# Summing gathered rows with four column groups of TensorE in one go

## The chip, the cores and the metric

The kernel runs on one core of a Trainium2 chip. The metric is the device time of one launch in microseconds; lower is better. A second kernel, with the change described below, is compared with it.

## What is computed

Two transformer blocks in a row on 256 tokens of width 1024, all in float32. The first block ends with a layer of product-key experts, and that is the part of interest. For every token each of 8 heads finds its 16 best of 16384 experts, takes their rows of a table `u`, and with the activated dot products as weights sums the rows of a second table `v`:

```
idx, gate = best 16 of 16384 per token and head
u = u_tab[idx]
act = gelu(einsum("td,thkd->thk", t, u))
vv = v_tab[idx]
out = einsum("thk,thkd->td", gate * act, vv)
```

That makes 256 x 128 rows of 4 KB of each table. The second block begins with its context: 256 further tokens go through a pooling mixer and a feed-forward layer and yield keys and values. The context doesn't depend on the experts, so the kernel does both at the same time.

## The kernel before

Each engine has its own program; they meet at semaphores. The experts stage runs from about 310 to 1120 us.

**The gathers.** A gather is an indirect DMA, issued by POOL (`po.indirect_dma_start`, line 2802), that brings one row of a table to each of 128 partitions: 512 KB. There are 512: 256 of `u`, one for each block of 128 tokens and each of its 128 choices, and 256 of `v`, in 8 sets `s` of 32 rows `m`. `fetched` (line 321) gives their order, `ROWS`: first 40 of `u`, then four of `v` and four of `u` in turn, and the last 40 are all `v`. They land in a ring of `NR` = 12 buffers. Gather n uses the buffer of gather n - 12, so before it issues, POOL waits until that one is used: on `v_u`, which VectorE raises after each dot product of a row of `u` (line 1851), or on `p_v`, which TensorE raises for each row of `v` (lines 2796 to 2801).

**The rows of v on TensorE** (`peer` in the TensorE program, line 1183). In a gathered row of `v` the 128 partitions are 32 tokens with 4 choices each. A matmul of 128 partitions by 32 columns, with the weights put on a diagonal by VectorE (`on_diagonal`, `v_wT`), sums the 4 choices into 32 tokens. `four_of` (line 332) sends row k to column group q = k % 4, that is to partitions 32q to 32q + 31 of the two banks `vb`. Each row needs two matmuls of 512 columns, i = 0 and i = 1, one for each bank. A matmul in float32 shows in the trace as two records, so a row has four, of the shape 128*32 by 128x512.

**The order of the work.** `turns` (line 386) writes out the sequence that all engines follow: gather n, then the use of gather n - 11, with the pieces of the top-k and of the weights at fixed places. `woven` (line 438) lets the context's program take a step at fixed counts of that sequence: its matmuls are of 128 by 128x256. TensorE works strictly in that order: if a row of `v` hasn't landed, the context behind it waits too. The rows of `v` are used in pairs, at each odd m: for i = 0 it waits for a row's landing and multiplies it, for both rows, and then for i = 1 the same two again.

```
elif what[0] == "use" and ROWS[what[1]][0] == "v" and ROWS[what[1]][2] % 2 == 1:
    ...
    for i in range(2):
        for k in range(m - 1, m + 1):
            n = NTH["v", s, k]
            q, c = four_of(k)
            if i == 0:
                pe.wait_ge(*at(f"d_r{n % NR}", 16 * (n // NR + 1)))
```

**Weights for the context** are loaded by SP into three slots of 2 MB (line 559), each as soon as TensorE has finished with a slot. The first loads of the context (`in_ctx`, line 607, then the constants `in_c_late`, the pooling weights and the feed-forward weights) wait for `a_sc` 10, the tenth eviction of the scores by ScalarE. After the experts come the normalisation of both token blocks, the pooling mixer and the rest of the second block, which TensorE's work fills.

Of the kernel before, what the change touches and what calls it, by code (L numbers as in the profile page):

```python
# [96 lines left out]
def program(nc, a, out):  # L97
# [32 lines left out]
    def at(name, n):  # L130

        sem = S[name]
        while name in GOES_ON:
            name, before = GOES_ON[name]
            n += before
        return sem, n
# [184 lines left out]
    def fetched():  # L321


        u = [("u", n // 128, n % 128) for n in range(256)]
        v = [("v", s, n) for s in range(8) for n in range(32)]
        both = [x for g in range(0, 256 - AHEAD, 4) for x in v[g:g + 4] + u[AHEAD + g:AHEAD + g + 4]]
        return u[0:AHEAD] + both + v[256 - AHEAD:]

    ROWS = fetched()
    NTH = {x: n for n, x in enumerate(ROWS)}  # L330

    def four_of(n):

        return n % 4, n // 4
# [314 lines left out]
    def _(pe):  # L649
        held, turn, ring8, kept = {}, [0], [list(range(7))], {}  # L650

        def take(name, reader, n, keep=False):


            while ring8[0][turn[0] % len(ring8[0])] in kept.values():
                turn[0] += 1
            i = ring8[0][turn[0] % len(ring8[0])]
            turn[0] += 1
            if keep:
                kept[name] = i  # L660
            if i in held:
                pe.wait_ge(*at(held[i][0], held[i][1]))
            held[i] = reader, n
            where[name] = ps[i]
            return ps[i]
# [6 lines left out]
        def mm(o, l, r, start, stop):  # L672
            return pe.matmul(o, l, r, start=start, stop=stop)  # L673

        def tr(o, i):
            n = i.shape[0]
            return pe.transpose(o, i, ident[0:n, 0:n])  # L677

        def c128(i):
            return slice(128 * i, 128 * i + 128)  # L680
# [11 lines left out]
        for t in range(2):  # L692
# [3 lines left out]
            for q in range(2):  # L696
                b = take(("hT", t, q), "v_hT", 2 * t + q + 1)
                for j in range(4):
                    k = tr(b[:, c128(j)], xn[:, t, c128(4 * q + j)])
# [7 lines left out]
        for kk in range(8):  # L707
            q = kk % 4
            k = mm(b[32 * q:32 * q + 32, 0:256], wg[:, kk, :], hT[:, kk, :], kk < 4, kk > 3)
# [5 lines left out]
        for t in range(2):  # L715
            k = mm(b[:, 32 * t:32 * t + 32], gsum[:, c128(t)], sums, True, True)
# [44 lines left out]
        for t in range(2):  # L761
            k = mm(b[:, 16 + 8 * t:24 + 8 * t], ones, GL[:, t, 0:8], True, True)
# [4 lines left out]
        for t in range(2):  # L767
            k = tr(b[0:8, c128(t)], CC[:, 8 * t:8 * t + 8])
# [63 lines left out]
        for d, r in ((0, mf), (1, mb)):  # L832
            for t in range(2):
                k = tr(b[:, 16 * d + 8 * t:16 * d + 8 * t + 8], r[:, c128(t)])
# [12 lines left out]
        for h in range(4):  # L847
            b = take(("kk", h), "v_kk", h + 1)
            for t in range(2):
                k = mm(b[:, c128(t)], KT[:, h, c128(t)], KT[:, h, c128(t)], True, True)  # L850
# [10 lines left out]
        for h in range(4):  # L861
# [3 lines left out]
            for t in range(2):  # L865
                k = mm(b[:, c128(t)], KT[:, h, c128(t)], QT[:, h, c128(t)], True, True)
            k.then_inc(S["p_kq"], 1)
        proj(7)
        for h in range(4):
            pe.wait_ge(*at("v_dt0", h + 1))  # L870
            b = take(("dd", h), "a_dd", h + 1)
            for i in range(4):
                k = tr(b[:, c128(i)], DT[:, 4 * h + i, :])
# [98 lines left out]
        for d in range(2):  # L972
            b = take(("s0", d), "a_vn", d + 1)
            for h in range(4):
                m = 4 * h + 3 * d
                k = mm(b[:, c128(h)], DT[:, m, :], BV[:, m, :], True, True)
# [4 lines left out]
        for d in range(2):  # L981
            pe.wait_ge(*at("a_vn", d + 1))
            b = take(("s1", d), "a_s1", d + 1)
            for h in range(4):
                k = mm(b[:, c128(h)], KD[:, 2 * h + d, :], VN[:, 4 * h + 3 * d, :], True, True)
            k.then_inc(S["p_s1"], 1)
        out_proj(1, 0, 1, yTm, 4, "p_wom")
        for d in range(2):
# [3 lines left out]
            for h in range(4):  # L992
                k = mm(b[:, c128(h)], KT[:, h, c128(u)], S1[:, 2 * h + d, :], True, True)
            k.then_inc(S["p_s2"], 1)
        out_proj(2, 1, 0, yTm, 4, "p_wom")
        for d in range(2):
            u = 1 - d
            b = take(("qs", d), "v_yg", 2 - d)
            for h in range(4):
                k = mm(b[:, c128(h)], QT[:, h, c128(u)], S1[:, 2 * h + d, :], True, True)  # L1000
# [3 lines left out]
            for h in range(4):  # L1004
                m = 4 * h + 2 * d + u
                k = mm(b[:, c128(h)], DT[:, m, :], BV[:, m, :], True, True)
# [3 lines left out]
        for t in range(2):  # L1010
            b = take(("go", t), "a_go", t + 1)
            for h in range(4):
                for d in range(2):
                    m = 4 * h + 2 * d + t
                    k = mm(b[:, c128(h)], PQ[:, m, :], VN[:, m, :], d == 0, d == 1)
# [167 lines left out]
        def peer():  # L1183
            for what in turns():
                if what[0] == "turn_rows":
                    s = what[1]
                    pe.wait_ge(*at("v_idx", 2 * s + 2))
                    tr(take(("iT", s), "v_iT", s + 1)[:, 0:128], chosen[s % 2]).then_inc(S["p_iT"], 1)
                elif what[0] == "turn_weights":
                    s = what[1]  # L1190
                    pe.wait_ge(*at("v_w", 2 * s + 2))
                    tr(take(("wT", s), "v_wT", s + 1)[:, 0:128], wt).then_inc(S["p_wT"], 1)
                elif what[0] == "use" and ROWS[what[1]][0] == "v" and ROWS[what[1]][2] % 2 == 1:
                    _, s, m = ROWS[what[1]]
                    if m == 1:
                        pe.wait_ge(*at("v_wT", s + 1))
                        if s == 0:
                            for i in (5, 6):
                                pe.wait_ge(*at(held[i][0], held[i][1]))
                        elif s == 4:  # L1200
                            pe.wait_ge(*at("v_add", 1))
                    for i in range(2):
                        for k in range(m - 1, m + 1):
                            n = NTH["v", s, k]
                            q, c = four_of(k)
                            if i == 0:
                                pe.wait_ge(*at(f"d_r{n % NR}", 16 * (n // NR + 1)))
                            o = mm(vb[i][32 * q:32 * q + 32, :], alone[s % 2][:, q, c, :], ring[n % NR][:, 512 * i:512 * i + 512],
                                   s % 4 == 0 and k < 4, s % 4 == 3 and k > 27)
                            if i == 1:  # L1210
                                o.then_inc(S["p_v"], 1)
                elif what[0] == "window_sums":
                    pe.wait_ge(*at("d_l", 48))
                    for n in range(2):
                        b = take(("zb", n), "a_sz", 1)
                        for e in range(2):
                            mm(b[:, 256 * e:256 * e + 256], ones, bands[2 * n + e][0], e == 0, False)
                            k = mm(b[:, 256 * e + 120:256 * e + 256], ones, bands[2 * n + e][1], False, e == 1)
                    k.then_inc(S["p_zb"], 1)
                yield what[0]  # L1220

        ring8[0] = [0, 1, 2, 3, 4, 7]
        woven(peer(), context())

        def r(ap):
            return ap.bitcast(FR)

        def mm3(o, lhs, rhs, start, stop):
            mm(o, r(lhs[0]), r(rhs[0]), start, False)
            mm(o, r(lhs[0]), r(rhs[1]), False, False)  # L1230
            return mm(o, r(lhs[1]), r(rhs[0]), False, stop)

        def both(pair, a0, n):
            return pair[0][:, a0:a0 + n], pair[1][:, a0:a0 + n]
# [25 lines left out]
        for g in range(4):  # L1260
            pe.wait_ge(*at("v_pl", g + 1))
            b = take(("pl", g), "v_px", 2 * g + 2)
            for j in range(2):
                for kk in range(2):
                    k = mm(b[:, 256 * j:256 * j + 256], w[:, 2 * g + kk, c128(j)], sqb[:, 2 * g + kk, :], kk == 0, kk == 1)
# [69 lines left out]
        for kk, hk in rows_first(True):  # L1335
            if hk == 0:
                row_there(rows_of[2], kk)
            k = mm3(b[hk], both(w, 256 * kk + 128 * hk, 128), both(ahx, 256 * kk, 256), kk == 0, kk == 7)
        k.then_inc(S["p_u"], 1)
        w = piece(35)  # L1340
        for t in range(2):
            b = take(("v", t), "a_vt", t + 1)
            for kk in range(8):
                k = mm3(b[:, 0:256], both(ahx, 256 * kk + 128 * t, 128), both(w, 256 * kk, 256), kk == 0, kk == 7)
# [96 lines left out]
        for q in range(2):  # L1441
            for t in range(2):
                pe.wait_ge(*at("v_dn", 12 + 4 * q))
                b = take(("y", q, t), "a_yo" if t == 0 else "v_yo", q + 1)
                for j in range(4):
                    k = tr(b[:, c128(j)], xT[:, 4 * q + j, c128(t)])
# [1423 lines left out]
```

## Time and profile before

| | us |
|---|---|
| median of the runs | 1681.04 |
| lowest and highest of 3 | 1680.31, 1688.94 |
| the profiled execution | 1669.39 |
| its span | 1667.6 |
| PE, DVE, ACT, POOL busy in it | 1478.8, 1106.1, 583.5, 824.9 |

The span is the time from the first to the last instruction on the core, in one execution that the hardware profiler took. The engines are PE (TensorE), DVE (VectorE), ACT (ScalarE), POOL (GpSimd) and SP. The busy time of PE includes the modelled tail of each matmul. "Idle before" is how long the engine stood still ahead of an instruction, and behind the arrow stands what ended it. The granted clock (PEclk) is a share of full speed, 2.4 GHz; the lower level is 1.2 GHz.

### The profile page before, as it was taken

To read this page: it belongs to the slowest core of one execution; us is meant where nothing else is said; L and a number is where in the kernel's file an instruction comes from. 1 tells how busy PE (TensorE), PEld (TensorE's weight loads), DVE (VectorE), ACT (ScalarE), POOL (GpSimd) and SP (SyncE) were. 2 spreads that over 40 slices of the span, in tenths; PEclk is the share of its full clock that TensorE was granted. 3 is DMA by queue.
4 is the path that set the end of the run, shared out by engine and by line. 5 is a ranking of instruction groups with operands and counts; after the bars stand their busy time and mean duration, and the time that the engine had idled before them with its cause. 6 is when DMAs were issued, how large, how long until landed. Compare 5 with 4: busy or idle time off the path is not lost.

```text
span 1667.6 us, 22193 instructions
## 1 busy us (share of the span) xinstructions
PE 1478.8 (89%) x8310; PEld 1059.6 (64%) x8310; DVE 1106.1 (66%) x2162; ACT 583.5 (35%) x847; POOL 824.9 (49%) x746
## 2 busy tenths in 40 slices
PE   8999999766565699999888885889999999999999
PEld 7997675654221266665443441438999896799987
DVE  4865633798488877877756675417886557468864
ACT  6653331211121222221100001127665454466652
POOL 0025230376767765656667777742675113036640
PEclk9999999987977899999799997999999999999999
DMA  7447860598999999999999999994555545635551
GB/s 281 152 151 301 318 253 26 210 389 304 393 407 371 409 401 402 402 403 403 401 401 394 409 396 402 406 396 161 171 187 190 189 182 222 243 111 202 176 191 38
DMA packets 154252, 477.15 MB, mean 286 GB/s; under 512 B 10017, under 2 KB 12321, under 8 KB 150945
## 3 DMA queue, kind: packets, MB, share of 16 engines
q0 software_dynamic: 73728, 268.47, 41.2%
q1 hardware_dynamic: 80416, 207.27, 34.0%
q8 instruction: 66, 1.08, 0.3%
q14 instruction: 42, 0.34, 0.1%
HBM read 474.65 MB, written 1.05 MB: 285 GB/s over the span
## 4 chain that ended last, share of the span: by engine, by line
PE 54%; DMA 13%; DVE 11%; POOL 10%; issue 5%; ACT 2%; DVEq 0%; ACTq 0%; POOLq 0%
PE ps L673 53%; DMA arena<-in_peer_v,cl 11%; POOL arena L2802 8%; DVE arena L1851 2%; PE ps L677 1%; POOL wring L2802 1%; DVE arena L1466 1%; DMA wring<-in_peer_v,cl 1%; DVE arena L1472 1%; DVE wring L1851 1%; DMA wring<-in_peer_u,arena 1%; DVE arena L1469 0%; DVE cvb L1472 0%; DVE arena L1781 0%; ACT arena L2190 0%
## 5 line engine op out<-in xcount | busy, mean ns | idle before, releaser
L673 PE MATMUL ps<-arena,wring 128*128 128x256 f32 (+2 forms) x2360 | 596.0, 488 | 106.0 <-DMA arena<-in_peer_v,cl 101.2
L673 PEld LDWEIGHTS ps<-arena,wring 128*128 128x128 f32 (+1 forms) x2360 | 333.0, 168 | 352.7 <-DMA arena<-in_peer_v,cl 179.7
L1851 DVE CUSTOM_DVE_ANT_0 arena<-arena 128x1024 f32<-128x1024 f32 x214 | 257.6, 1226 | 134.8 <-DMA arena<-in_peer_u,arena 131.9
L2802 POOL DMA_INDIRECT arena<-in_peer_u,arena x214 | 240.0, 1121 | 192.4 <-DVE arena L1809 78.2
L2802 POOL DMA_INDIRECT arena<-in_peer_v,cl x214 | 229.2, 1071 | 77.3 <-issue 60.4
L673 PE MATMUL ps<-hhl,wh 128*128 128x256 f32 (+1 forms) x1056 | 252.4, 323 | 1.2 <-POOL hhl L2812 0.7
L2190 ACT ACT_TABLE_LOAD x64 | 82.1, 1283 | 392.9 <-DVE arena L1851 266.1
L1466 DVE TENSOR_TENSOR wl<-wring,wh 128x2048 fp32r<-128x2048 f32 (+1 forms) x76 | 168.1, 2212 | 60.0 <-ACT wh L2193 58.2
L673 PE MATMUL ps<-hhl,wl 128*128 128x256 f32 x704 | 198.7, 282 | 0.0
L673 PEld LDWEIGHTS ps<-hhl,wh 128*128 128x128 f32 x1056 | 175.8, 190 | 19.5 <-POOL hhl L2812 2.5
L2193 ACT ACTIVATE wh<-wring 128x2048 fp32r<-128x2048 f32 (+1 forms) x78 | 146.1, 1874 | 70.7 <-PE ps L673 68.9
L673 PE MATMUL ps<-ahl,wh 128*128 128x512 f32 (+1 forms) x496 | 164.2, 363 | 0.1
L2820 POOL TENSOR_TENSOR cvb<-cvb 128x256 f32<-128x256 f32 x44 | 122.3, 2779 | 82.3 <-ACT cvb L2190 82.3
L1472 DVE SCALAR_TENSOR_TENSOR cvb<-ps,vec,cvb 128x255 f32<-128x255 f32 x264 | 127.5, 483 | 38.9 <-ACT cvb L2190 30.2
L673 PEld LDWEIGHTS ps<-hhl,wl 128*128 128x128 f32 x704 | 134.2, 191 | 0.0
L2756 POOL TENSOR_TENSOR arena<-arena,cl 128x256 f32<-128x256 f32 x56 | 43.7, 780 | 157.4 <-PE ps L673 154.1
L673 PEld LDWEIGHTS ps<-arena 128*128 128x128 f32 (+1 forms) x708 | 85.9, 191 | 48.0 <-issue 20.9
L673 PE MATMUL ps<-arena 128*128 128x128 f32 (+4 forms) x708 | 98.0, 290 | 20.5 <-ACT arena L2193 11.7
L2190 ACT ACTIVATE cvb<-ps,vec 128x256 f32<-128x256 f32 x132 | 74.5, 565 | 106.5 <-PE ps L673 86.8
L2193 ACT ACTIVATE arena<-ps 128x512 f32<-128x512 f32 (+1 forms) x97 | 56.0, 577 | 142.4 <-PE ps L673 101.8
L673 PEld LDWEIGHTS ps<-ahl,wh 128*128 128x128 f32 x496 | 93.6, 189 | 15.8 <-issue 0.5
L673 PE MATMUL ps<-ahl,wl 128*128 128x256 f32 x352 | 98.8, 281 | 0.0
(257 smaller groups left out, 2025.4 us busy)
## 6 DMA issues: line engine op xcount, KB each, us to landing
wring<-in_ups SPq DMA_DIRECT2D x33, 2048.0 KB, 9.2
wring<-in_ada SPq DMA_DIRECT2D x24, 2048.0 KB, 9.9
wring<-in_ffn_w_down SPq DMA_DIRECT2D x12, 2048.0 KB, 9.0
wring<-in_w_in SPq DMA_DIRECT2D x8, 2048.0 KB, 8.3
wring<-in_ffn_w_down SPq DMA_DIRECT2D x6, 1536.0 KB, 7.6
wring<-in_peer_wq SPq DMA_DIRECT2D x4, 2048.0 KB, 16.1
wring<-in_attn_w_qkv SPq DMA_DIRECT2D x4, 2048.0 KB, 8.4
wring<-in_w_out SPq DMA_DIRECT2D x2, 2048.0 KB, 9.7
```

Of the source, the lines that this page charges most:

```text
L673: return pe.matmul(o, l, r, start=start, stop=stop)
L677: return pe.transpose(o, i, ident[0:n, 0:n])
L1466: return ve.tensor_tensor(o, x, y, op)
L1472: return ve.scalar_tensor_tensor(o, x, s, y, op0, op1)
L1851: ve.tensor_tensor_reduce(out=o, in0=o, in1=h2[:, t, :], scale=1.0, scalar=0.0, op0=MUL, op1=ADD, accum_out=dots[j % 2][:, k:k + 1]).then_ ...
L2190: return ac.activation(o, x, f, bias=bias, scale=scale, accum_out=accum)
L2193: return ac.activation(o, x, ACT.Copy)
L2756: k = po.tensor_tensor(OTs[l % 2][:, m:m + 2, :], AM[:, m:m + 2, :], bc(cl[:, o:o + 128], 2, 1), MUL)
L2802: po.indirect_dma_start(out=ring[n % NR], out_offset=None, in_=table, in_offset=bass.IndirectOffsetOnAxis(ap=which, axis=0)).then_inc(S[f" ...
L2820: seq(po.tensor_tensor(cv[:, 0, :], cv[:, 0, :], cv[:, 1, :], MUL))
```

## The change

The rows of `v` are used four at a time, at m = 3, 7, and so on, in place of two at a time, at each odd m. For i = 0 the four matmuls of a group follow each other, one in each column group, each behind its own landing; then the four for i = 1. The numbers of gathers, matmuls and increments are the same, and so is every other engine's program.

```
-                elif what[0] == "use" and ROWS[what[1]][0] == "v" and ROWS[what[1]][2] % 2 == 1:
+                elif what[0] == "use" and ROWS[what[1]][0] == "v" and ROWS[what[1]][2] % 4 == 3:
                     _, s, m = ROWS[what[1]]
-                    if m == 1:
+                    if m == 3:
                         pe.wait_ge(*at("v_wT", s + 1))
...
                     for i in range(2):
-                        for k in range(m - 1, m + 1):
+                        for k in range(m - 3, m + 1):
                             n = NTH["v", s, k]
                             q, c = four_of(k)
                             if i == 0:
```

On TensorE the context's steps keep their counts, so what stood between two pairs now stands ahead of the four. Here at the first rows of `v` (`arena` and `wring` are the memory that holds the ring; 32x512 are the rows of `v`, 128x256 the queries of the experts, 128x128 their scores; counts are matmuls, each two records):

```order
 L673 MATMUL ps<-arena,wring 128x256 x8
-L673 MATMUL ps<-arena,wring 32x512 x4
-L673 MATMUL ps<-arena 128x128 x4
-L673 MATMUL ps<-arena,wring 32x512 x4
+L673 MATMUL ps<-arena 128x128 x4
+L673 MATMUL ps<-arena,wring 32x512 x8
 L673 MATMUL ps<-arena,wring 128x256 x8
 L673 MATMUL ps<-arena,wring 32x512 x8
 L673 MATMUL ps<-arena,wring 128x256 x8
 L673 MATMUL ps<-arena 128x128 x4
```

The first pair has moved behind the scores and joins the second.

And where the context's feed-forward layer begins (128x256), on TensorE, before:

```order
L677 MATMUL ps<-cbase,gt 128x128
L673 MATMUL ps<-arena,wring 128x256 x16
L673 MATMUL ps<-arena,wring 32x512 x4
L673 MATMUL ps<-arena,wring 128x256 x8
L673 MATMUL ps<-arena,wring 32x512 x4
L673 MATMUL ps<-arena,wring 128x256 x16
```

and with the change:

```order
L677 MATMUL ps<-cbase,gt 128x128
L673 MATMUL ps<-arena,wring 128x256 x24
L673 MATMUL ps<-arena,wring 32x512 x8
L673 MATMUL ps<-arena,wring 128x256 x24
L673 MATMUL ps<-arena,wring 32x512 x2
L673 MATMUL ps<-wring 32x512 x2
```

Per eight gathers there were 16 matmuls of context, a pair, 8 of context, a pair; now there are 24 of context and then the four.

## Rows read from the trace of the kernel before

**Rows 1.** The page, part 2: busy share of PE and of DMA in 40 slices, tenths
```profile
PE   8999999766565699999888885889999999999999
...
DMA  7447860598999999999999999994555545635551
```

**Rows 2.** The page, part 4: the chain that ended last, shares of the span
```profile
PE 54%; DMA 13%; DVE 11%; POOL 10%; issue 5%; ACT 2%; DVEq 0%; ACTq 0%; POOLq 0%
```

**Rows 3.** Stretches: length; busy PE, PEld, DVE, ACT, POOL; clock, DMA share, GB/s
```profile
400.00:410.00 10.00, 10.00 (x55) 5.34 (x57) 8.21 (x25) 1.19 (x2) 5.31 (x6) 1.00 0.70 235
410.00:420.00 10.00, 9.05 (x48) 4.72 (x38) 5.84 (x17) 3.09 (x6) 7.86 (x8) 1.00 0.96 338
420.00:500.00 80.00, 49.99 (x148) 17.20 (x146) 54.08 (x118) 17.36 (x28) 56.05 (x49) 0.81 1.03 403
510.00:520.00 10.00, 4.99 (x16) 1.99 (x16) 9.41 (x28) 0.00 (x0) 8.09 (x7) 0.94 0.87 273
530.00:580.00 50.00, 30.47 (x93) 10.72 (x90) 40.44 (x92) 11.42 (x19) 38.72 (x38) 0.87 1.03 409
585.00:790.00 205.00, 201.74 (x900) 136.76 (x900) 155.54 (x368) 50.76 (x85) 128.75 (x120) 1.00 1.03 402
```

**Rows 4.** The tile in_peer_v: gathers of v, from issue to landing
```profile
DMA to landing us min/median/max: 5.1/10.4/20.7
```

**Rows 5.** Timeline of PE: start, us, what, records
```profile
13.13 1.07 PE L673 MATMUL ps<-arena 128*32 128x256 f32 x16 [1.00 <-DVE arena L1466]
...
1073.67 1.94 PE L673 MATMUL ps<-arena,wring 128*32 128x512 f32 x16
1075.41 1.89 PE L673 MATMUL ps<-wring 128*32 128x512 f32 x8
```

**Rows 6.** PE's groups by shape, 585 to 790: records, busy us, mean ns
```profile
L673 PE MATMUL ps<-arena,wring 128*128 128x256 f32 x670 | 151.6, 383 | 0.0
L673 PE MATMUL ps<-arena,wring 128*32 128x512 f32 x188 | 45.8, 604 | 3.1 <-DMA arena<-in_peer_v,cl 3.1
L673 PE MATMUL ps<-wring 128*32 128x512 f32 x40 | 10.2, 599 | 0.0
```

**Rows 7.** Timeline at the first rows of v: the scores on PE, POOL's issues
```profile
402.39 1.16 PE L673 MATMUL ps<-arena 128*128 128x128 f32 x8
...
402.72 0.94 POOL L2802 DMA_INDIRECT arena<-in_peer_u,arena  x1 [4.58 <-PE ps L673]
403.96 0.94 POOL L2802 DMA_INDIRECT arena<-in_peer_u,arena  x1 [0.30 <-issue]
405.65 0.94 POOL L2802 DMA_INDIRECT arena<-in_peer_u,arena  x1 [0.75 <-PE ps L673]
```

**Rows 8.** Timeline of SP's queue, from 410: the context's first load
```profile
417.18 0.37 SPq L607 DMA_DIRECT2D arena<-in_ctx  x1
```

**Rows 9.** Timeline of PE and POOL, 485 to 500
```profile
485.85 9.01 PE L673 MATMUL ps<-arena,wring 128*32 128x512 f32 x24 [2.18 <-DMA arena<-in_peer_v,cl]
...
490.31 1.21 POOL L2802 DMA_INDIRECT arena<-in_peer_u,arena  x1 [0.30 <-issue]
491.83 1.14 POOL L2802 DMA_INDIRECT arena<-in_peer_u,arena  x1 [0.30 <-issue]
495.12 1.02 POOL L2802 DMA_INDIRECT arena<-in_peer_u,arena  x1 [2.15 <-PE ps L673]
496.45 1.87 POOL L2802 DMA_INDIRECT arena<-in_peer_u,arena  x1 [0.30 <-issue]
498.63 1.99 POOL L2802 DMA_INDIRECT arena<-in_peer_v,cl  x1 [0.30 <-issue]
```

**Rows 10.** Timeline at the end of the stage: POOL's last gathers, PE's last row
```profile
1106.19 0.94 POOL L2802 DMA_INDIRECT arena<-in_peer_v,cl  x1 [0.30 <-issue]
1107.43 0.94 POOL L2802 DMA_INDIRECT arena<-in_peer_v,cl  x1 [0.30 <-issue]
...
1117.55 1.90 PE L673 MATMUL ps<-arena,wring 128*32 128x512 f32 x6 [0.68 <-DMA arena<-in_peer_v,cl]
```

More of the change, by code:

```diff
@@ L1192, in peer @@
                     tr(take(("wT", s), "v_wT", s + 1)[:, 0:128], wt).then_inc(S["p_wT"], 1)
-                elif what[0] == "use" and ROWS[what[1]][0] == "v" and ROWS[what[1]][2] % 2 == 1:
+                elif what[0] == "use" and ROWS[what[1]][0] == "v" and ROWS[what[1]][2] % 4 == 3:
                     _, s, m = ROWS[what[1]]
-                    if m == 1:
+                    if m == 3:
                         pe.wait_ge(*at("v_wT", s + 1))
@@ L1202, in peer @@
                     for i in range(2):
-                        for k in range(m - 1, m + 1):
+                        for k in range(m - 3, m + 1):
                             n = NTH["v", s, k]
```

## The prediction

> **What bounds the kernel now.** I read the page first. In its 40 slices of 41.7 us the DMA row stands at 9 from the eleventh to the twenty-seventh, about 417 to 1126 us [rows 1]; this is the experts stage, and only there does the changed code run. The chain that ended last names TensorE for 54%, but also DMA, chiefly rows of `peer_v`, for 13% and POOL for 10% [rows 2]; so the stage has to be read by itself, from the table of stretches [rows 3]. The busy PE of 201.74 out of 205 us from 585 to 790 looks like a bound. The same row gives DMA 1.03 and 402 GB/s, and the two rows that decide are those where PE is not full: 420 to 500 has PE at 49.99 of 80 us and the same 1.03 and 403 GB/s, and 530 to 580, with gathers alone, has PE at 30.47 of 50 us, 1.03 and 409 GB/s. Where weights are loaded beside gathers the rate is 402 or 403, whether PE is full or not. So I take the DMA engines as the bound of the whole stage, with PE just below them from 585 to 790. Only three short windows are clearly under that rate: 235, 338 and 273 GB/s [rows 3].
>
> One gathered row (128 partitions of 4 KB, 524 KB) takes 524/409 = 1.28 us of the DMA engines. From issue to landing a row of v takes 5.1 us at least and 10.4 in the median [rows 4]. The first figure is the empty queue: 5.1/1.28 = 4 rows must be outstanding to keep the DMA engines full; the median says that 8 are. The ring has 12.
>
> **What the change makes of a group of four.** Instructions are neither added nor removed; four rows still give 16 records on PE (8 matmuls, each recorded twice) and four increments of `p_v`. What changes is which stand next to each other. Eight records of one pair take 1.89 us, from 1075.41 [rows 5]; sixteen records that stand together with all rows landed take 1.94 us, from 1073.67 [rows 5], because the second pair lies in other columns and runs beside the first. The gates' matmul, sixteen records over four column groups, confirms it: it took 1.07 us, from 13.13 [rows 5], where 16 records of the same 256 columns that follow one another, 0.226 us apart [rows 6], would take 3.6. So before, two pairs that met in a backlog were already four abreast. The gain is where a piece of the context's work stood between them. From 585 to 790 nearly all are such: 228 records (57 rows) took 45.8 + 10.2 = 56.0 us, 0.98 us a row, 3.93 us for four [rows 6]. As a four they should take 1.94, so PE gets back 2.0 us for each of 57/4 = 14 groups, **28 us** in this stretch.
>
> **What that is worth, term by term**, against the profiled execution (1669.39 us, span 1667.6).
>
> 1. *585 to 790.* The 28 us fall beside a DMA queue that is full. A cycle of eight gathered rows took 205/14.25 = 14.4 us. PE's own work in it becomes 24 matmuls of 128x256, 48 records at 151.6/670 = 0.226 us, 10.9 us [rows 6], plus 1.94, in all 12.8. Before it was 10.9 + 3.9 = 14.8, which is why PE looked full. Now PE waits about 1.6 us per cycle for rows. I take 0. Below it: if the stretch came up from 402 to the 409 GB/s of bare gathers, 205 x 7/409 = 3.5 us; above: nothing, since PE gets only lighter here. The bare windows 420 to 500 are the nearer row, hence 0.
>
> 2. *The first four rows of v.* POOL stood still 4.58 us for the first pair and issued again at 402.72 [rows 7]. In the new order the scores (8 records, 1.16 us [rows 7]) go ahead of it and the four take 1.9 us, so this issue comes about 1.9 us later. POOL then needs 1.24 us per issue, 0.94 plus 0.30 [rows 7], so it hardly catches up; but the third and fourth slots, which before came 0.75 us late, are now there. Net lag about 1.5 us into a DMA queue that is nearly empty. Against it: SP's loads for the context wait for the scores' last eviction and went out at 417.18 [rows 8]. On PE, scores come one place earlier each time and the rows of v between take one 1.9 us instead of two, so these loads start 1.5 to 2 us earlier and fill the same hole with other bytes. Taken as 0; bounds -1.5 and +1.9.
>
> 3. *485 to 515.* A backlog of 24 records, 9.01 us, ended on PE at 494.86; a piece of context stood ahead of its last pair, and POOL waited 2.15 us for that pair, until 495.12, after two issues at 490.31 and 491.83 for the slots of the pair before [rows 9]. As a four behind the context both pairs are done at about 494.86 - 1.9 = 492.9. The two issues then come at 492.9 rather than 490.31, and the third two issues later (2.7 us by [rows 9]), at 495.6 rather than 495.12: 0.5 us late. After that POOL sets the pace itself (1.3 to 2.3 us an issue), and the thin window at 510 follows from it, so the lag counts: +0.5, bounds -0.6 and +1.5.
>
> 4. *All other groups.* With the first pair used only when the fourth row is in, its two slots come back two landings, 2.6 us, later; where the context stood between the pairs, its 16 records (3.6 us) come on top. What hides it: the next row for such a slot must land nine landings after the fourth, 11.5 us; it needs 5.1 to land and PE needs about 2 for the four, so 4.4 us are left (before 7.0). If PE is later than 4.4 us, the cover is gone and the DMA queue runs dry by the difference. 0, bounds 0 and +3 (a few groups by a microsecond).
>
> 5. *The end of the stage.* Last rows: POOL issues every 1.24 us to 1107.43, the landing is 10 us later, PE starts on the last row at 1117.55 and is done after 1.90 us [rows 10]. With four, the last row still has two matmuls of its own one after the other; the other three lie beside them. 0, at most +0.3.
>
> 6. *Clock.* PE waits more, so its granted clock may fall in places (0.81 from 420 to 500 [rows 3]); it costs PE time that is not on the path, unless it is low when the next stage begins. 0, at most +2.
>
> The sum is +0.5, with bounds from -5.6 to +8.7 if all fell together, so 1669.9 for the profiled execution. The runs shown have a median of 1681.04, 11.65 us above it, and run from 1680.31 to 1688.94. The forecast for the median is **1681.5**. About 0.5%, 8.4 us, is what a measurement of this kernel can tell from no change.
>
> The Trainium skill, "DMA: Bandwidth & Descriptors", Specifications, puts the fabric's ceiling at 435 GB/s and the limit of HBM for one core at about 358. The trace disagrees with the second (402 to 409 sustained) and shows nothing over 409 in these stretches. By the first there would be 8% left for a faster PE to claim, an estimate of 205 x (1 - 402/435) = 16 us; this is a rival below, worked out there without it.
>
> **Rivals.**
> *Faster, PE was the bound* from 585 to 790 and DMA only kept step. For: 201.74 of 205 us busy, POOL waits for PE. Against: rows at the same rate with PE at 62%. It would give the rate of bare gathers, 3.5 us, and as PE also frees slots sooner, the three thin windows: (168 + 65 + 130) x 10/403 = 9.0 us. Together 12.5: **1668.5**.
> *Much faster*: PE's relief is taken in full measure until something else binds. The 28 us are the end, DVE's 155.54 of 205 us is no obstacle; half of it, 14 us, gives **1667**. It would need a rate of 205/191 x 402 = 431 GB/s, which no window has. The Trainium skill's ceiling of 435 is what would allow it.
> *Slower, the ring is too short.* Late slots empty the queue. It decides at fewer than four rows outstanding, that is PE over 4.4 us late. The place is 800 to 1060 us, where few weights cover, some 25 groups. If half of them lose 1 us, +12: **1693**. Against: the median of 10.4 us says eight outstanding.
> *It does nothing*: if PE ran no more than two groups at once. The sixteen records in 1.94 us speak against it; the time would be the same 1681.5.
>
> **How the numbers follow.** No change, with the last rival, 0.64; its own range is -5.6 to +8.7 about the median of before, 1675 to 1690. The two faster ones 0.15 and 0.07; slower 0.14. Faster by over 0.5% 0.22, within 0.64, slower 0.14. The range 1668 to 1690 takes in the first faster case and leaves out most of the second and the slower one, under 2 in 10.
>
> **What the changed profile would show.** PE busy between 585 and 790 down from 201.74 to about 175 to 180 us; matmuls of 128x32 taking about 0.5 us a row in place of 0.98; DMA share 1.03 and 402 GB/s as before; POOL's first issue after the standstill near 404.6 in place of 402.72; SP's `in_ctx` near 415.5; the last gather landing within 5 us of 1117.5. Wrong if the rate of the stretch rises over 409, or if windows of 10 us between 800 and 1060 fall well below 400 GB/s.

## The result, and the profile after

| | us |
|---|---|
| before, median of 20 runs (lowest and highest) | 1681.1 (1674.81, 1691.36) |
| with the change, median of 20 runs | 1689.01 (1683.19, 1694.18) |
| ratio, with its 95% interval | 1.0042 (1.0027 to 1.0058) |
| the profiled execution, and its span | 1685.32, 1683.5 |

The change costs 7.9 us by the medians. That is inside the forecast range, and just within the 8.4 us (0.5%) that the prediction took as no change. But the interval of the ratio excludes no difference, and the direction is that of the rival "slower", which had the chance 0.14 for a loss over 0.5%.

The page of the changed kernel: busy time of the engines, the slices that [rows 1] showed, and the chain of [rows 2].

```profile
PE 1461.0 (87%) x8310; PEld 1047.3 (62%) x8310; DVE 1106.2 (66%) x2162; ACT 583.7 (35%) x847; POOL 833.9 (50%) x746
...
PE   8999999756666699899787876789999999999999
...
DMA  7447860698999999999999999995555546635451
...
PE 45%; POOL 16%; DVE 12%; DMA 10%; issue 9%; ACT 2%; another core or an unknown queue 1%; ACTq 0%; DVEq 0%; POOLq 0%
```

PE is 17.8 us less busy than before (1478.8), and yet the run is longer: on the chain PE has gone from 54% to 45% and POOL from 10% to 16%. The DMA row has its 9 in the same slices as before, up to the twenty-seventh; a slice is now 42.1 us in place of 41.7, so that the last of them ends at about 1136 us in place of 1126. Now the stretches of [rows 3], and two that were not shown there:

```profile
400.00:410.00 10.00, 9.75 (x62) 5.94 (x63) 6.28 (x22) 0.79 (x2) 5.21 (x5) 1.00 0.57 193
410.00:420.00 10.00, 6.71 (x26) 3.16 (x24) 6.71 (x17) 3.09 (x6) 7.93 (x7) 1.00 0.93 338
420.00:500.00 80.00, 48.42 (x146) 15.14 (x146) 53.15 (x116) 17.36 (x28) 55.07 (x49) 0.77 1.03 402
510.00:520.00 10.00, 4.87 (x20) 1.95 (x20) 9.41 (x27) 0.00 (x0) 7.87 (x8) 1.00 0.90 273
585.00:790.00 205.00, 194.23 (x922) 137.84 (x921) 154.88 (x369) 49.30 (x83) 130.83 (x122) 0.98 1.03 397
800.00:1060.00 260.00, 193.92 (x715) 88.96 (x716) 167.24 (x385) 24.78 (x38) 184.70 (x173) 0.90 1.01 391
1060.00:1116.00 56.00, 47.69 (x212) 20.23 (x209) 14.75 (x30) 11.88 (x23) 38.87 (x40) 0.97 0.99 373
```

The last two stretches in the first profile of before:

```profile
800.00:1060.00 260.00, 203.72 (x740) 94.31 (x741) 170.80 (x391) 22.37 (x34) 193.00 (x182) 0.89 1.02 401
1060.00:1116.00 56.00, 53.17 (x238) 22.67 (x236) 9.88 (x22) 11.87 (x23) 34.56 (x36) 1.00 1.02 401
```

It is tempting to read the whole loss from that. But a profile is one execution, and the one shown of before (1669.39 us) lay 12 us under its own median. So the kernel before was run and profiled once more, unchanged ("before again" below). Expected of it:

> The kernel before unchanged, for a second profile: the first was of an execution of 1669 us, under all but the very fastest of its runs. If that execution was a lucky one, this profile shows thin windows of the DMA queue as well (10 us under 380 GB/s) between 500 and 1110 us, four to eight of them, and a span of 1675 to 1685 us.

It took 1683.37 us, span 1681.6. The same three stretches of that execution:

```profile
585.00:790.00 205.00, 201.13 (x901) 135.92 (x902) 154.99 (x368) 50.67 (x84) 131.65 (x122) 1.00 1.02 397
800.00:1060.00 260.00, 201.49 (x726) 92.51 (x726) 168.45 (x386) 22.41 (x34) 189.77 (x177) 0.91 1.01 394
1060.00:1116.00 56.00, 51.54 (x227) 22.61 (x227) 11.37 (x26) 11.89 (x23) 36.39 (x38) 0.97 1.00 386
```

The kernel before, too, runs at 397, 394 and 386 GB/s on an ordinary execution. Of windows of 10 us below 380 GB/s between 500 and 1110, the first profile of before had 3, the second 14 (four to eight were expected), the changed kernel 11. Its PE is busy for 1487.6 us and has 58% of its chain, POOL 11%: against it the changed kernel's PE is 26.6 us less busy. So most of what the two first traces differ by isn't the change. What is left can be read from the last gather that POOL issues. The rows of the tile `in_peer_v` (median duration in the middle, then the first and the last start), of before, of before again and of the changed kernel:

```profile
L2802 POOL DMA_INDIRECT arena<-in_peer_v,cl x214: 933/937/1989, 380.4 to 1107.4; - x107
```

```profile
L2802 POOL DMA_INDIRECT arena<-in_peer_v,cl x214: 936/941/1992, 379.2 to 1119.6; - x107
```

```profile
L2802 POOL DMA_INDIRECT arena<-in_peer_v,cl x214: 932/941/1987, 379.3 to 1125.9; - x107
```

From before again to the changed kernel the last gather is 6.3 us later, with the same start; the medians differ by 7.9. One profile of each can't show that these 6.3 us are the change, since the two profiles of before differ by 12.2 us in the same number. What the rows do show is the place: from the last gather to the end of the span it is 560.2, 562.0 and 557.6 us, no longer in the changed kernel than before. So whatever is lost is lost within the experts stage, and the mean granted clock (0.945 and 0.947) is no part of it.

### The profile page after: what moved, and what is told of

The parts are those of the page before. It is cut to its first block, busy times and chain, and to the rows that moved or that the text cites. A ratio compares the mean times of both kernels' runs of the same rounds, so it can differ in the third digit from the quotient of the medians.

```text
span 1683.5 us, 22193 instructions
## 1 busy us (share of the span) xinstructions
PE 1461.0 (87%) x8310; PEld 1047.3 (62%) x8310; DVE 1106.2 (66%) x2162; ACT 583.7 (35%) x847; POOL 833.9 (50%) x746
## 4 chain that ended last, share of the span: by engine, by line
PE 45%; POOL 16%; DVE 12%; DMA 10%; issue 9%; ACT 2%; another core or an unknown queue 1%; ACTq 0%; DVEq 0%; POOLq 0%
PE ps L673 43%; POOL arena L2802 13%; DMA arena<-in_peer_v,cl 5%; DMA wring<-in_peer_v,cl 3%; DVE arena L1851 3%; POOL wring L2802 2%; PE ps L677 2%; DMA wring<-in_peer_u,arena 1%; DVE arena L1466 1%; DVE arena L1472 1%; DVE wring L1851 1%; DVE arena L1781 1%; DVE cvb L1472 1%; DMA arena<-in_peer_u,arena 1%
## 5 line engine op out<-in xcount | busy, mean ns | idle before, releaser
L673 PE MATMUL ps<-arena,wring 128*128 128x256 f32 (+2 forms) x2360 | 583.1, 486 | 118.7 <-DMA arena<-in_peer_v,cl 91.9
L673 PEld LDWEIGHTS ps<-arena,wring 128*128 128x128 f32 (+1 forms) x2360 | 322.7, 167 | 341.8 <-DMA arena<-in_peer_v,cl 189.3
L2802 POOL DMA_INDIRECT arena<-in_peer_u,arena x214 | 249.1, 1164 | 214.6 <-DVE arena L1809 77.5
L2802 POOL DMA_INDIRECT arena<-in_peer_v,cl x214 | 225.7, 1055 | 83.4 <-issue 62.6
```

What stands on the lines that cost most here:

```text
L2802: po.indirect_dma_start(out=ring[n % NR], out_offset=None, in_=table, in_offset=bass.IndirectOffsetOnAxis(ap=which, axis=0)).then_inc(S[f" ...
```

## The experiments

Ratios are to runs of before on the same chip, whose medians were 1682.6, 1682.4 and 1683.4 us in the three batches. The theory was that slots of the ring come back too late (the expectations call the wait for later landings theory A, the place behind the context theory B, and any cause that isn't the slots theory C). It has two parts, since the change makes a slot wait for the landing of the fourth row, and it also puts both pairs behind context that stood between them. The rivals: the order of the matmuls within a group, and the place beside the context alone.

**Slots late, matmuls unmoved.** On the kernel before, the matmuls stay where they are and the first pair's increments are given with the second's:

```
-                            if i == 1:
-                                o.then_inc(S["p_v"], 1)
+                            if i == 1 and m % 4 == 3:
+                                o.then_inc(S["p_v"], 2)
```

> The kernel before with its matmuls in pairs at their own places, but the semaphore p_v is raised for all four rows only with the second pair. So the late slots of the change alone, without its gain on PE and without moving a matmul. Theory A (late slots cost, PE's lighter load gives a part back): slower than before by at least as much as the change, 1.004 to 1.008. If late slots cost nothing and the change was slow through the place of its matmuls: 0.999 to 1.001.

Measured over 6 runs: 1704.05 us, ratio 1.0109 (1.0079 to 1.0139). That is some 18 us by the ratio and 20.7 by the medians, and more than was expected. Of its profile the stretch, the tile and POOL's waits from 380 to 1150 us (in all, times, longest):

```profile
800.00:1060.00 260.00, 200.01 (x725) 93.91 (x725) 157.76 (x375) 23.67 (x34) 178.03 (x165) 0.89 0.98 372
```

```profile
L2802 POOL DMA_INDIRECT arena<-in_peer_v,cl x214: 935/941/1987, 380.1 to 1147.3; - x107
```

```profile
POOL arena L2802 <- PE ps L673: 96.5, 31, 7.9
```

372 GB/s from 800 to 1060 in place of 394, the last gather 27.7 us later than in before again, and POOL waits 96.5 us for PE on these slots, where before again has 59.4, and 11.7 more on the two in `wring`. Nothing about PE's work was changed, so this is the price of late slots alone. Not all of it arises where PE has gaps: by the timelines of POOL the gathers are 7.9 us behind those of before again at 547 us, 20.4 at 729 and 27.7 at the end, so nearly half of the lag comes in the stretch in which PE is full. The price is well over what the change costs: the change must also win something.

**What PE's relief is worth.** Gathers of `v` bring 2 KB to each partition in place of 4, into the first half of the buffer, once on before and once on the changed kernel. The table is addressed in half rows for this and the second half of the buffer keeps what was there, so the result is no longer the sum; the instructions stay:

```
-            po.indirect_dma_start(out=ring[n % NR], out_offset=None, in_=table,
+            cols_of = 512 if kind == "v" else 1024
+            po.indirect_dma_start(out=ring[n % NR][:, 0:cols_of], out_offset=None, in_=table if kind == "u" else table.rearrange("n (two d) -> (n two) d", two=2),
```

> The kernel before with gathers of v that bring only 2 KB per partition in place of 4 (the first half of the buffer is new, the second half holds what was there), so the values are not the sum; all instructions stay. It takes 67 MB off the DMA engines. If they are the bound of the stage: up to 167 us less at 402 GB/s, but POOL's 512 issues of 1.24 us and PE's 202 us from 585 to 790 stay, so 60 to 130 us less, ratio 0.92 to 0.965. If PE is the bound from 585 to 790 and only kept company by DMA, 20 to 60 us less.

> The same with the changed kernel. With the DMA engines relieved, PE's relief of 28 us should show where PE is the bound: 10 to 28 us faster than e7, if the change's PE gain is real and was only hidden behind the DMA. If POOL's pace or the ring binds then: within 5 us of e7, or slower.

Before with half rows: 1671.8 us (4 runs), ratio 0.9912 (0.9882 to 0.9942). Changed, with half rows: 1658.18 (4 runs), 0.9859 (0.983 to 0.9888). With so few runs the two measures differ: half rows gave before 10.6 us by the medians and 14.8 by the ratio, and the change gave 13.6 or 8.9 us on top; the two intervals just overlap. The stretches, of the first and then of the second:

```profile
585.00:790.00 205.00, 199.58 (x885) 133.77 (x882) 152.92 (x367) 50.05 (x84) 125.58 (x119) 0.98 0.92 330
800.00:1060.00 260.00, 196.49 (x738) 96.45 (x740) 167.24 (x383) 21.96 (x33) 199.11 (x175) 0.86 0.86 299
```

```profile
585.00:790.00 205.00, 189.66 (x933) 132.42 (x922) 166.99 (x394) 52.44 (x89) 151.67 (x131) 0.98 0.98 361
800.00:1060.00 260.00, 189.24 (x753) 93.42 (x755) 153.37 (x343) 24.44 (x37) 199.24 (x178) 0.88 0.86 299
```

Two things follow. 67 MB less (256 gathers of 128 rows, 2 KB each), which at 402 GB/s would be 167 us, bought 11 to 15 us, less than either case of the expectation; so the DMA engines are not the one bound of this stage. In the profile the last gather starts at 1118.9 us, where before again has 1119.6. From 585 to 790 the DMA share has come off 1.02 to 0.92, and PE is still busy 199.58 of 205: there PE holds the pace. And with that load off, the change is 9 to 14 us the better, at 361 GB/s against 330: PE's relief is worth time as soon as rows land early enough. With half rows they do, and from the first to the second POOL's waits for PE fall from 41.8 + 10.3 us (`arena` and `wring`) to 18.7 + 1.2.

**Where the pairs stand, and what a group waits for.** Four kernels cross the two parts. In the first the group stands where the change puts it, but each pair does its i = 0 and i = 1 before the next pair, so the first two slots don't wait for the third and fourth landings:

```
-                        for k in range(m - 1, m + 1):
+                    for first in (m - 3, m - 1):
+                      for i in range(2):
+                        for k in range(first, first + 2):
```

> The four rows stay at the place of the change (behind the context), but are done as two pairs, so the first two slots of the ring come back without waiting for the landing of the third and fourth row. Theory A, late slots empty the DMA queue, and the wait for the fourth landing is a main part: half or more of the 0.42% comes back, ratio to before 1.000 to 1.002. Theory B, it is the context that now stands ahead of the first pair that delays the slots: the ratio stays at 1.003 to 1.005. Theory C, the loss has nothing to do with slots (clock, or POOL and VectorE disturbing each other): 1.003 to 1.005 as well, and POOL's long waits for PE are then as in the changed kernel.

Measured: 1682.7 us (12 runs), 1.0001 (0.9981 to 1.0022). The loss of the change is gone, as theory A expected, though all eight matmuls still stand behind the context. This kernel also changes the order of the matmuls within the group; that late slots cost without any such change is what the first experiment showed.

In the next two the context's step waits while a group of four is incomplete, so that the group stands ahead of it; once with the change, once with the pairs of before:

```
-                if n == half:
+                used = ROWS[n - 18] if 18 <= n < 530 else ("u", 0, 0)
+                if used[0] == "v" and used[2] % 4 != 3:
+                    continue
+                if half and n >= half:
```

> The change, with every step of the context that would fall within a group of four held until the four rows are used; so the four stand ahead of the context's matmuls and not behind them. Theory A (the wait for the fourth landing alone): still slower than before, 1.002 to 1.005. Theory B (context ahead of the first pair): the loss goes, ratio 0.998 to 1.001. Theory C: 1.003 to 1.005.

> The kernel before, pairs, with the context's steps held in the same way, so that both pairs of a group stand together ahead of the context. PE gets the four groups abreast wherever it is behind, and no slot waits for a later landing. Theories A and B: not slower than before, 0.996 to 1.001. If PE's relief of 28 us in 585 to 790 were worth anything it shows here: under 0.997. If the ratio is over 1.002, delaying the context's steps has a price of its own and e2 has to be read against this run.

Four ahead of the context: 1683.95 (12 runs), 1.0020 (1.0001 to 1.0039). Pairs ahead of it: 1676.14 (12 runs), 0.9967 (0.995 to 0.9984). This was the one kernel clearly ahead of before, so it was run again in another batch:

> e3 again (pairs, both ahead of the context's matmuls), to see whether its gain stands: ratio 0.995 to 0.999.

1680.85 (12 runs), 0.9988 (0.9971 to 1.0006). Together:

| | behind the context | ahead of it |
|---|---|---|
| four by four, i = 0 of all first | 1.0042 (the change) | 1.0020 |
| in pairs | 1.0001 | 0.9967, again 0.9988 |

Down each column, waiting for the fourth landing costs 0.3 to 0.5%. Along the first row, standing behind the context costs 0.2%, though those two intervals overlap. The first part is the larger.

The same question from the other side, four ahead of the context but row by row, each slot given back as its row is done, and no i = 0 standing side by side:

```
-                    for i in range(2):
-                        for k in range(m - 1, m + 1):
+                    for k in range(m - 3, m + 1):
+                        for i in range(2):
```

> As e2, four rows ahead of the context, but row by row: both matmuls of a row, then the next row, so that a row's slot needs its own landing alone, and rows in other columns still run abreast when PE is behind. Theory A (the wait for a later landing is what costs): at least as good as e3, ratio 0.994 to 0.998. If pairs are the right size (the second matmul of a row after its neighbour's first fills the time between landings), worse than e3: 0.998 to 1.001.

1680.4 (12 runs), 0.9987 (0.997 to 1.0004). Against 1.0020 for the same place with the change's loops (another batch) it is 0.3% the better, though the two intervals just overlap. Its slots come back sooner and its matmuls have less to overlap with, which fits the slots outweighing the overlap here too. It isn't better than pairs in that place (0.9967 and 0.9988), as theory A alone would have it.

**Smaller groups.** Each row used at its own m, first in the place of before, then with the hold ahead of the context:

```
-                elif what[0] == "use" and ROWS[what[1]][0] == "v" and ROWS[what[1]][2] % 2 == 1:
+                elif what[0] == "use" and ROWS[what[1]][0] == "v":
...
-                        for k in range(m - 1, m + 1):
+                        for k in range(m, m + 1):
```

> The other way: each row of v is used as soon as it has landed, at its own place in the sequence, alone. Slots come back earliest. Theory A: as fast as before or faster, 0.996 to 1.000, though PE has less to run abreast where context stands between rows (up to 4 rows one after another, 1.7 us each). If PE is the bound from 585 to 790, this is clearly slower there: PE's work per eight rows would be 10.9 + up to 6.9 us = 17.8 against 14.4 available, up to 14 x 3.4 = 48 us, ratio up to 1.03.

> Each row by itself as it lands, with the context's steps held until the group of four is used, so that rows meet in PE's backlog and run abreast. It gives slots back earliest and takes from PE as little as the four. By theory A alone: as good as e3 or better, 0.993 to 0.998. e5, which did the same from the fourth row's place, gave 0.9987; if the two matmuls of a row in one column group, one after the other, are what made e5 worse than pairs, this gives 0.998 to 1.001 too.

One by one: 1686.57 (12 runs), 1.0023 (1.0003 to 1.0044), slower than theory A had it and far from the 1.03 of the other case. With the hold: 1681.69 (12 runs), 0.9992 (0.9975 to 1.001). In the first, PE has no gap left from 585 to 790:

```profile
585.00:790.00 205.00, 205.00 (x896) 134.56 (x895) 149.63 (x356) 48.19 (x81) 126.14 (x118) 1.00 1.03 397
```

So it seems that the slots that come back soonest are paid for with PE's time there. That one by one is worse for this reason is argued from this row and from the half rows; the hold, which lets rows meet, brought it back to no difference.

**A shorter ring.** On before, `NR = 11` with the order of the work kept, which makes every slot one landing late:

> The kernel before with a ring of 11 buffers and the same sequence, so each slot is asked for one landing (1.28 us) earlier. Theory A says that the slack of the ring is used up somewhere in every execution: slower than before by 0.3 to 0.8% (the change made half of v's slots 2.6 us late, a quarter of all; here all are 1.28 us short). If the ring has slack as the prediction held (8 rows outstanding, 4 needed): ratio 0.999 to 1.001.

1684.87 (12 runs), 1.0013 (0.9999 to 1.0028). The interval just reaches no difference, and theory A had 0.3 to 0.8%. One landing late, evenly, costs little. In the change half of `v`'s slots, a quarter of all, are two landings late and the others on time, which is less in the mean; what the fours have on top is that the delay is uneven and, in their first pair, includes the context. These two were not told apart here. So lateness as such doesn't give the price; how it is spread does.

## Why the number held and the reasons did not

The forecast was 1681.5 us with a range to 1690, and 1689.01 lies within it. That is luck in part: a loss of some 18 us that the sum had at 0 (term 4) and a gain of some 11 us that it also had at 0 (term 1) nearly cancelled. By its own terms:

*Term 1, 585 to 790, PE's relief worth 0.* Wrong. The argument was that two rows with PE at 62% had the same 402 to 409 GB/s, so DMA alone must set the pace. They show that DMA can be full elsewhere, not that PE isn't the pace in this stretch. Late slots alone cost some 18 us (1.09%), the change 0.42%, and the difference, 0.67% or 11 us, is what the change's matmuls win back; the half rows gave 9 to 14. This is a difference of two kernels and not a measurement by itself (from the two intervals, an estimate, it is 6 to 17 us), but both stand clear of the 0 of the sum, and of its bound of 3.5 us. It is the gain over the whole stage; how much of it falls between 585 and 790 was not measured apart.

The saving on PE was itself about a third of what was worked out. PE's groups by shape in the changed kernel, as in [rows 6]:

```profile
L673 PE MATMUL ps<-arena,wring 128*128 128x256 f32 x679 | 155.2, 388 | 0.9 <-issue 0.7
L673 PE MATMUL ps<-arena,wring 128*32 128x512 f32 x200 | 36.9, 601 | 3.5 <-DMA arena<-in_peer_v,cl 2.9 <-issue 0.6
L673 PE MATMUL ps<-wring 128*32 128x512 f32 x40 | 12.7, 600 | 2.8 <-DMA wring<-in_peer_v,cl 2.8
```

240 records are 60 rows in 36.9 + 12.7 = 49.6 us, 0.83 us a row: 0.15 less than 0.98, where 0.5 less was predicted. The timeline of PE shows why:

```profile
655.36 1.04 PE L673 MATMUL ps<-wring 128*32 128x512 f32 x2 [0.58 <-DMA wring<-in_peer_v,cl]
656.64 0.62 PE L673 MATMUL ps<-wring 128*32 128x512 f32 x1 [0.23 <-DMA wring<-in_peer_v,cl]
656.64 0.62 PE L673 MATMUL ps<-arena,wring 128*32 128x512 f32 x2
656.66 1.02 PE L673 MATMUL ps<-wring 128*32 128x512 f32 x2
```

And of before again, at the same place, a pair whose rows had both landed:

```profile
656.89 1.91 PE L673 MATMUL ps<-wring 128*32 128x512 f32 x8
```

In this four of the changed kernel the first row's matmul, two records, stands alone for 1.04 us, since the rows come 1.3 us apart, and PE begins the group as soon as the first is in. The sixteen records in 1.94 us of [rows 5] had all rows landed. Nor did PE fall to 175 to 180 us of 205; it was 194.23.

*Term 4, all other groups, late slots hidden.* Wrong, and the step that decides the sign. It was priced at 0, at most +3; by themselves late slots cost some 18 us. The working held that a ring of 12, with eight rows outstanding where four are needed, left 4.4 us of cover. That took a median of outstanding rows for every group. But some groups come later than that, and then POOL is stopped, as here between 979 and 983; the second fence is the stretch around it:

```profile
978.34 0.94 POOL L2802 DMA_INDIRECT arena<-in_peer_v,cl  x1 [0.30 <-issue]
982.49 0.94 POOL L2802 DMA_INDIRECT arena<-in_peer_u,arena  x1 [3.21 <-remote]
983.73 0.94 POOL L2802 DMA_INDIRECT arena<-in_peer_u,arena  x1 [0.30 <-issue]
984.97 0.94 POOL L2802 DMA_INDIRECT arena<-in_peer_u,arena  x1 [0.30 <-issue]
986.21 0.94 POOL L2802 DMA_INDIRECT arena<-in_peer_u,arena  x1 [0.30 <-PE ps L673]
```

```profile
980.00:990.00 10.00, 8.32 (x32) 3.85 (x31) 6.70 (x17) 3.18 (x5) 5.99 (x6) 0.83 0.84 285
```

POOL stands 3.21 us and then issues four in a row, 1.24 us each. By the order of the gathers what it stood for is the slot of a group's first row; the trace doesn't name what released it. Before again stands here too, at the same gather and even a little longer, so this row shows what follows a standstill and not what the change adds:

```profile
976.15 0.93 POOL L2802 DMA_INDIRECT arena<-in_peer_u,arena  x1 [3.85 <-remote]
```

In the changed kernel all four slots are there at once, but POOL issues hardly faster than DMA moves: 1.24 us against the 1.28 of the prediction, so what a standstill takes from the queue comes back at 0.04 us a gather. That is, as I read it, what the working left out: it saw this at the first rows of v (term 2) and then gave every group its full 4.4 us of cover again. Over the stage the waits have become fewer and longer. POOL's waits for PE on the slots in `arena`, of before again (with those in `wring`) and of the changed kernel, from 380 to 1150 us (in all, times, longest):

```profile
POOL arena L2802 <- PE ps L673: 59.4, 39, 4.5
...
POOL wring L2802 <- PE ps L673: 11.7, 11, 3.2
```

```profile
POOL arena L2802 <- PE ps L673: 60.0, 24, 6.1
POOL arena L2802 <- remote: 24.1, 15, 3.8
```

In `arena` the sum for PE is the same, but in 24 waits for 39; on `wring` the changed kernel has 0.3 us. ("remote" stands where the trace lacks the event that released POOL; before again has 17.2 us of those in `arena`.) Gather by gather, by the slot that each one needs, POOL stands some 74 us for slots of `v` in 48 waits in before again, 74 in 32 waits in the changed kernel, and 100 in 33 with late slots alone. So the changed kernel's late slots don't show in the sum of these waits: what they add, the lighter PE takes off again, as it seems. What shows the term is the kernel with the late slots alone, and the one that takes the group in pairs at the same place (1.0001).

*Term 2, the first rows of v.* The order was right, the sizes near. POOL's issue came at 403.51 rather than the 404.6 forecast, 0.79 us later than in the first profile of before, and SP's load at 415.04 (forecast 415.5):

```profile
396.47 0.94 POOL L2802 DMA_INDIRECT arena<-in_peer_v,cl  x1 [0.30 <-issue]
403.51 0.94 POOL L2802 DMA_INDIRECT arena<-in_peer_u,arena  x1 [6.10 <-PE ps L673]
...
415.04 0.37 SPq L607 DMA_DIRECT2D arena<-in_ctx  x1
```

The standstill grew from 4.58 to 6.10 us, 400 to 410 thinned from 235 to 193 GB/s (42 x 10 = 0.42 MB, 1 us at 402), and 410 to 420 is at 338 in both. Within its bounds. Against before again the standstill grew by 1.9 us, as forecast:

```profile
401.20 1.00 POOL L2802 DMA_INDIRECT arena<-in_peer_u,arena  x1 [4.19 <-PE ps L673]
```

But SP's load went out at 415.66 there, so it comes 0.6 us earlier with the change and not 1.5 to 2.

*Term 3, 485 to 515.* The lag was larger than worked out. POOL, before again and then with the change:

```profile
493.73 1.40 POOL L2802 DMA_INDIRECT arena<-in_peer_u,arena  x1 [1.78 <-PE ps L673]
```

```profile
494.96 0.94 POOL L2802 DMA_INDIRECT arena<-in_peer_u,arena  x1 [2.53 <-remote]
496.20 0.94 POOL L2802 DMA_INDIRECT arena<-in_peer_u,arena  x1 [0.30 <-issue]
497.44 1.80 POOL L2802 DMA_INDIRECT arena<-in_peer_u,arena  x1 [0.30 <-issue]
```

The first row is the third of four gathers of `u` and answers to the last; the forecast for it was 495.6. Not all of this lag arises here: the first gather of `v` into `wring` ahead of it started at 486.06 in before again and at 490.08 with the change. The two windows after it, before again:

```profile
500.00:510.00 10.00, 7.17 (x24) 3.29 (x23) 9.73 (x16) 0.00 (x0) 8.48 (x6) 0.83 0.97 354
510.00:520.00 10.00, 4.98 (x14) 1.73 (x11) 9.45 (x27) 0.00 (x0) 7.87 (x8) 0.84 0.86 297
```

With the change they have 326 and 273 GB/s: 28 + 24 = 52 GB/s over 10 us, at 403 GB/s 1.3 us. The term was +0.5 with +1.5 as its bound.

*Term 5, the end of the stage.* Right for the length: PE's run on the last rows takes 1.90 us as in [rows 10]. The last landing itself was forecast within 5 us of 1117.5 and came 14.8 us later, of which 12.2 us separate the two profiles of before as well (by their last gathers).

```profile
1132.32 1.90 PE L673 MATMUL ps<-arena,wring 128*32 128x512 f32 x10 [0.19 <-DMA arena<-in_peer_v,cl]
```

*Term 6, the clock.* 0.77 in place of 0.81 from 420 to 500, as in before again, and a mean of 0.947 between the 0.945 and 0.952 of before. Right.

*The rivals.* "Slower, the ring is too short" had the mechanism, but it was priced for one place and half the groups, and it set nothing against PE's relief. "PE was the bound" had the other half. Each was taken as a case that excludes the other; both are true in one kernel, and the time is their difference: 18 lost and some 11 won. The rival that rested on a rate of 431 GB/s is not borne out: the long stretches shown of these runs have 409 at most, and PE's relief was worth time below that rate. The Trainium skill, "DMA: Bandwidth & Descriptors", Specifications, gives a ceiling of 435 GB/s; no stretch shown here reached it.

The check in the prediction, "wrong if windows between 800 and 1060 fall well below 400 GB/s", was met (285 GB/s from 980 to 990), but met by the kernel before as well (317 in before again, 358 from 990 to 1000 in the first profile). It was made from a single profile, and an unusually fast one.

**What stays open.** Pairs ahead of the context measured 0.9967 and 0.9988 against before. Both point the same way and the second interval includes no difference, so a gain of 0.1 to 0.3% is likely but not settled. (0.9967 is also the lowest of several kernels tried, which favours a lucky draw.) In that kernel POOL waits more for VectorE's use of `u`:

```profile
POOL arena L2805 <- DVE arena L1854: 43.7, 13, 6.7
POOL arena L2805 <- PE ps L676: 22.1, 26, 3.5
```

22.1 us for PE in place of 59.4, but 43.7 for VectorE in place of 9.1: the wait has moved to the engine next in line. What it would be worth to relieve both was not tried.

## What to carry to other kernels

When buffers of a ring are used in groups, ask when the first one of the group comes free, not how many are outstanding in the median: work that the first could have done must not stand behind the landing of the last, least of all where, as here, the issuer needs about as long for a transfer (1.24 us) as the transfer takes (1.28). A cheaper instruction sequence on a nearly full engine and an earlier return of its buffers are two prices to be measured apart, since a change may trade one for the other; here giving slots back late with nothing else changed, and halving the bytes on both kernels, did that in three runs. And profile the kernel before twice: a stretch of 401 GB/s in one execution and 386 to 394 in the next is more than the effect looked for.

## What was not expected of the hardware

A DMA share of 1.02 to 1.03 was taken for a resource that sets the pace. With 67 MB fewer the stretch from 585 to 790 ran at a share of 0.92 and the program gained 11 to 15 us, where the bytes alone would give 167: here a full share said that the queue had work, not that the end waited for it.

The same kernel spreads from 1674.81 to 1691.36 us over 20 runs, 1%, with the granted clock all but the same (0.952 in the fastest profile, 0.945 in the other). The two profiles of before differ in where gathers thin out; what makes them differ was not found.

Matmuls in other column groups overlap across a pair's border only while all data are there: sixteen records of 128x32 by 512 took 1.94 us, eight took 1.89 and two alone 1.04. So four abreast cost the same as two, and where PE is behind, two pairs that follow each other run abreast without any wait for a later landing.
